# Gated heads of an HGRN2 block: six binary levels of decayed products as three groups of four quarters, and the sums of k and v moved behind a dense panel

## What is computed

```
log_f = log_sigmoid(zf);  k = sigmoid(-zf);  q = silu(zq)
S_t = diag(f_t) S_{t-1} + k_t v_t^T
o_t = S_t^T q_t                # then RMSNorm over the head, times silu(zo)
```

## Time and profile before

| | |
|---|---|
| median of 3 runs | 1657.83 us (1657.72 to 1658.1) |
| the profiled execution | 1658.33 us, of which its span is 1656.6 us |
| busy in the span | PE 1620.1, DVE 837.7, ACT 826.4, POOL 708.4 us |
| stage of the heads | from 103 us to about 345 us |
| one turn of the loop over heads | 32.72 us |

### The profile page before, as it was taken

The page is one execution under the profiler, slowest core; times in us unless marked ns, Lnnn a source line. Parts: engine busy times, 40 slices in busy tenths (PEclk is TensorE's granted clock), DMA queues, the critical chain, the costliest instruction groups (busy, mean ns, idle before and its releaser), DMA issues.

```text
span 1656.6 us, 21578 instructions
## 1 busy us (share of the span) xinstructions
PE 1620.1 (98%) x7677; PEld 1341.8 (81%) x7677; DVE 837.7 (51%) x1279; ACT 826.4 (50%) x1102; POOL 708.4 (43%) x934
## 2 busy tenths in 40 slices
PE   7999999999999999999999999999999999999997
PEld 6888888888888888888887788888888887788875
DVE  3566666631124212121256758358357348679676
ACT  6467777752334313132346645445345355654764
POOL 7453333346666454555565534634635632000000
PEclk9999999999999999999999999999999999999999
DMA  6231221123333333333333222422422313232311
GB/s 206 77 88 52 63 76 57 49 68 106 101 102 102 91 100 101 90 101 94 97 93 85 77 64 76 115 64 77 113 56 81 110 61 88 82 91 81 97 58 61
DMA packets 251096, 142.95 MB, mean 86 GB/s; under 512 B 6161, under 2 KB 249618, under 8 KB 251026
## 3 DMA queue, kind: packets, MB, share of 16 engines
q1 hardware_dynamic: 251026, 142.00, 29.7%
HBM read 139.89 MB, written 2.10 MB: 86 GB/s over the span
## 4 chain that ended last, share of the span: by engine, by line
PE 71%; DVE 6%; ACT 2%; issue 1%; DVEq 0%; ACTq 0%
PE bank L801 19%; PE bank L802 18%; PE bank L809 18%; PE bank L792 2%; PE bank L793 2%; PE bank L794 2%; PE bank L1126 1%; PE bank L1109 1%; PE bank L1108 1%; PE bank L1107 1%; DVE xT L2147 1%; DVE w_lo L2444 1%; PE bank L1252 1%; PE bank L1254 1%; PE bank L1253 1%
## 5 line engine op out<-in xcount | busy, mean ns | idle before, releaser
L772 POOL TENSOR_TENSOR w_lo<-raw,w_hi 128x256 fp32r<-128x256 f32 x896 | 697.3, 811 | 668.8 <-ACT w_hi L1340 668.5
L1340 ACT ACTIVATE w_hi<-raw 128x1024 fp32r<-128x1024 f32 x264 | 277.4, 1055 | 507.8 <-PE bank L809 454.4
L801 PE MATMUL bank<-h_hi,w_hi 128*128 128x512 f32 x1252 | 497.0, 397 | 0.0
L802 PE MATMUL bank<-h_lo,w_hi 128*128 128x512 f32 x1252 | 487.8, 390 | 0.0
L809 PE MATMUL bank<-h_hi,w_lo 128*128 128x512 f32 x1252 | 309.8, 389 | 0.0
L801 PEld LDWEIGHTS bank<-h_hi,w_hi 128*128 128x128 f32 x1252 | 235.1, 188 | 54.2 <-issue 6.0
L802 PEld LDWEIGHTS bank<-h_lo,w_hi 128*128 128x128 f32 x1252 | 235.1, 188 | 52.0 <-issue 4.1
L809 PEld LDWEIGHTS bank<-h_hi,w_lo 128*128 128x128 f32 x1252 | 235.0, 188 | 49.3 <-issue 0.5
L2147 DVE TENSOR_TENSOR xT<-xT,bank 128x512 f32<-128x512 f32 x103 | 68.3, 685 | 205.9 <-PE bank L809 156.9
L2172 DVE SCALAR_TENSOR_TENSOR fr<-bank,rstd 128x512 f32<-128x512 f32 x32 | 22.1, 692 | 133.6 <-PE bank L809 127.9
L801 PE MATMUL bank<-f_hi,w_hi 128*128 128x512 f32 x224 | 87.1, 389 | 0.0
(11 more groups left out here) (430 smaller groups left out, 2711.1 us busy)
## 6 DMA issues: line engine op xcount, KB each, us to landing
raw<-in_w_ff SPq DMA_DIRECT2D x64, 512.0 KB, 4.0
raw<-in_w_in SPq DMA_DIRECT2D x56, 512.0 KB, 3.8
raw<-in_m_w_in SPq DMA_DIRECT2D x48, 512.0 KB, 3.9
raw<-in_r_w_in SPq DMA_DIRECT2D x24, 512.0 KB, 3.8
raw<-in_m_w_out SPq DMA_DIRECT2D x16, 512.0 KB, 3.4
raw<-in_r_w_out SPq DMA_DIRECT2D x16, 384.0 KB, 3.2
raw<-in_w_up_b SPq DMA_DIRECT2D x8, 512.0 KB, 4.1
raw<-in_w_out SPq DMA_DIRECT2D x8, 512.0 KB, 3.9
```

The source lines that it names most:

```text
L772: ins = pool.tensor_tensor(w_lo[:, s, part], raw[:, s, part], w_hi[:, s, part].bitcast(F32), ALU.subtract)
L801: pe.matmul(dst, w_hi[:, s, c], hi[:, k, :], start=(k == 0), stop=False)
L802: pe.matmul(dst, w_hi[:, s, c], lo[:, k, :], start=False, stop=False)
L1340: act.activation(w_hi[:, p % RING, :], raw[:, p % RING, :], ACT.Copy).then_inc(hi_ready[p % RING], 1)
```

## The change

- `GROUPS = [2, 8, 32]` takes the place of the six levels above 1. A group splits an aligned run of 4h tokens into four quarters. The keys of the first three quarters are decayed to the end of their own quarter (`sk`, in place, 384 of 512 columns); of the queries there are three variants side by side (`sq3`): quarters 1 to 3 referred to the end of quarter 0 (3h of 4h columns), quarters 2 and 3 referred to the end of quarter 1 (2h), quarter 3 referred to the end of quarter 2 (h). Together 192 columns in a block.
- PE makes one product of 192 columns for a block in each group, in two parts of two blocks; each part takes a whole bank (`GROUP_BANK`, `GROUP_TURN`). The transposes of `kd` come after the last group.
- DVE writes each part into `sd` with three predicated copies, of 3h, 2h and h columns in each run, under a mask of one byte for a quarter that is broadcast over its columns. 24 copies a head, 10 before.
- The products of `kT` and `vT` are a function of their own, `head_sums`, in bank 6, between the panels 2 and 3 of the next head; `head_states` runs within the next head's `head_prepare`, after its first exponents. The head's output is in bank 4, its sum of squares in bank 5.
- Exponents and exponentials are made in place in `sk`, `sq3` and `kd`; `ee` and `qk` are gone. `sk` is cleared once. The mask tables are smaller.

```diff
-LEVELS = [1, 2, 4, 8, 16, 32, 64]
-NMASK = 8
+GROUPS = [2, 8, 32]
+NG = len(GROUPS)
+N_LEVEL = 2 + 2 * NG
-JOBS = [1, 2, 4, 8, "k", 16, 32, 64, "q"]
+JOBS = [1, 2, 8, "k", 32, "q"]
+GROUP_BANK = {0: (6, 4), 1: (5, 6), 2: (7, 4)}
+GROUP_TURN = {0: (0, 1), 1: (1, 1), 2: (1, 2)}
-H_AUX = {4: 2, 5: 3, 6: 2, 7: 3}
+H_AUX = {4: 4, 5: 4, 6: 3, 7: 2}
...
 # PE
-                for m in range(2, NMASK):
...
-                    pe.wait_ge(qk_made, i * NJ + JOBS.index(h) + 1)
-                    for n in range(NT):
...
-                        mm = pe.matmul(dst.rearrange("p (b t) -> p b t", t=h), qk[:, m - 2, c], right, start=True,
-                                       stop=True, skip_group_check=True)
-                    mm.then_inc(level_done, 1)
-                    if m == 4:
-                        free(5, 1)
...
+                def group(g):
+                    pe.wait_ge(qk_made, i * NJ + JOBS.index(GROUPS[g]) + 1)
+                    for part in range(2):
+                        b = GROUP_BANK[g][part]
+                        free(b, GROUP_TURN[g][part])
+                        for n in range(2 * part, 2 * part + 2):
+                            at = (n - 2 * part) * PAIR
+                            mm = pe.matmul(bank[b][:, at:at + PAIR], sk[:, g, n * P:(n + 1) * P], sq3[:, g, n, :],
+                                           start=True, stop=True, skip_group_check=True)
+                        mm.then_inc(level_done, 1)
+
+                group(0)
+                group(1)
+                group(2)
                 free(5, 2)
+                pe.wait_ge(qk_made, i * NJ + JK + 1)
+                for c in range(NT - 1):
+                    mm = pe.transpose(bank[5][:, c * P:(c + 1) * P], kd[:, c * P:(c + 1) * P], ident[:])
+                mm.then_inc(kd_turned, 1)
+
+            def head_sums(i):
+                aux_released(pe, 6, AUX_H[6] + 2, i, H_AUX[6])
                 pe.wait_ge(kT_made, i + 1)
                 for c in range(NT - 1):
-                    mm = pe.matmul(bank[5][:, c * P:(c + 1) * P], kT[:, c, :], vT[:, c, :], start=True, stop=True,
+                    mm = pe.matmul(bank[6][:, c * P:(c + 1) * P], kT[:, c, :], vT[:, c, :], start=True, stop=True,
                                    skip_group_check=True)
                 mm.then_inc(kv_done, 1)
...
                 head_levels(i)
                 head_in(i + 1, 2)
+                head_sums(i)
                 head_in(i + 1, 3)
                 head_values(i)
...
 # ACT
+                            e = sk[:, g, :].rearrange("p (b c) -> p b c", c=4 * JOBS[j])[:, :, 0:3 * JOBS[j]]
+                            act.activation(e, e, ACT.Exp)
+                            e = sq3[:, g].rearrange("p n c -> p (n c)")
+                            act.activation(e, e, ACT.Exp).then_inc(decay_made, 1)
...
 # DVE, exponent(j)
+                        dve.tensor_tensor(e, c[:, :, :, h - 1:h].to_broadcast([P, S // (4 * h), 3, h]), c, ALU.subtract)
...
+                        for part, dst in variants(sq3[:, GROUPS.index(h)], h):
...
+                            ins = dve.tensor_tensor(dst, later(cn, h, part),
+                                                    end.to_broadcast([P, NT, P // (4 * h), w]), ALU.subtract)
+                        ins.then_inc(expo_made, 1)
...
 # DVE, weigh(j)
+                        dve.tensor_tensor(e, e, blocks(kk[:], h)[:, :, 0:3, :], ALU.mult)
+                        for part, e in variants(sq3[:, g], h):
+                            ins = dve.tensor_tensor(e, e, later(qq, h, part), ALU.mult)
+                        ins.then_inc(qk_made, 1)
                 exponent(1)
                 for j in range(NJ):
+                    if j == 0 and before is not None:
+                        head_states(before)
                     if j + 2 < NJ:
                         exponent(j + 2)
                     weigh(j)
...
 # DVE, head_masks
+                def group(g, part):
...
+                    dve.wait_ge(level_done, i * N_LEVEL + 3 + 2 * g + part)
...
+                    for quarter in range(3):
+                        w = (3 - quarter) * h
+                        dst = sd[:, n:n + 2, :].rearrange("p n (g s) -> p n g s", s=4 * h)[:, :, :, (quarter + 1) * h:]
+                        src = both[:, :, at:at + groups * w].rearrange("p n (g s) -> p n g s", s=w)
...
+                        turn()
+                        ins = dve.copy_predicated(dst, mask, src)
+                        if quarter < 2:
+                            ins.then_inc(mask_turn, 1)
+                            turns += 1
+                            dve.wait_ge(mask_turn, i * M_TURNS + turns)
+                    ins.then_inc(aux_free[b], 1)
+                    if (g, part) != (NG - 1, 1):
+                        dve.wait_ge(aux_free[b], AUX_H[b] + GROUP_TURN[g][part] + 1 + i * H_AUX[b])
```

More of the change, by code:

```diff
@@ L963, in head_sum @@
             def head_sum(i):
[L964 removed]
+                aux_released(pe, 5, AUX_H[5] + 3, i, H_AUX[5])
                 pe.wait_ge(hsq_made, i + 1)
[L966 removed]
+                pe.matmul(bank[5][:], ones[:], hsq, start=True, stop=True).then_inc(hss_done, 1)
             def up(i, n):
@@ L1927, in _ @@
             dve.tensor_copy(mask_d[:], maskf[:, 0:1, :])
-            for n in range(NT):
-                dve.tensor_copy(mask4[:, 1:, n * 64:(n + 1) * 64], maskf[:, 1:, 0:64])
+            dve.tensor_copy(mask4[:, 0:NMASK, :], maskf[:])
             for n in range(NT):
@@ L1983, in head_prepare, with variants, later @@
                 link(dve.tensor_tensor_scan(cum[:], keep[:], lf[:], 0.0, ALU.mult, ALU.add))
+                def variants(t, h):
+                    g = P // (4 * h)
+                    at = 0
+                    for part in range(3):
+                        w = (3 - part) * h
+                        yield part, t[:, :, at:at + g * w].rearrange("p n (g s) -> p n g s", s=w)
+                        at += g * w
+                def later(ap, h, part):
+                    return ap.rearrange("p n (g s) -> p n g s", s=4 * h)[:, :, :, (part + 1) * h:4 * h]
                 def exponent(j):
@@ L2079, in head_masks @@
-                assert turns == M_TURNS
+                for g in range(NG):
+                    group(g, 0)
+                    group(g, 1)
+                assert turns == M_TURNS, turns
             def head_states(i):
                 dve.wait_ge(kv_done, i + 1)
-                link(dve.tensor_copy(state[:, 0, :], bank[5][:, 0:P]))
-                link(dve.scalar_tensor_tensor(state[:, 1, :], state[:, 0, :], eq[:, P - 1:P], bank[5][:, P:2 * P],
+                link(dve.tensor_copy(state[:, 0, :], bank[6][:, 0:P]))
```

165 lines of the change are left out of this document (68 added, 97 removed).

## The result

The changed kernel takes 1678.32 us as a median (1677.35 to 1678.67 in 4 runs), 1.0122 of the kernel before (95% interval 1.0109 to 1.0135). The forecast was 1679.6, in a range from 1667 to 1690. The profiled execution has a span of 1676.3 us against 1656.6.

The account below looks back on a forecast made before the run. PE, busy 32.47 of a head's 32.72 us, was taken as the bound. Seven steps at +2.3 us (16.1) plus +5.7 in the last head gave +21.8 us: 1679.6 us as a median, range 1667 to 1690.

Parts of the forecast that it names:

- PE's own work: Level products on PE: 48 passes (5.21 us) become 24 (3.8 us), 1.4 us less in a head.
- The masks: DVE's copies into sd: 18 short for six, a part 1.46 us (1.63 at h = 2) with gaps, ending at 13.0.
- Dear copies: Rival on DVE's masks: each of the 18 copies takes 0.445 us, a part 1.87; 1690 us, chance 0.12.
- cheap masks: Rival on DVE's masks: no gap between copies, parts 0.93 to 1.1 us; 1661 us, chance 0.05.
- PE's stalls in the levels: PE waits in the groups for banks that DVE's copies must free: 2.9 us a head, longest 0.95.
- The rival that never waits: In the levels: copies keep up with PE, whose whole saving of 1.4 us a head comes out; 1647 us, chance 0.04.
- the rival of a slow clock in each head: Stalls in the levels drop PE to half clock in each head, +11 us more; 1691 us, chance 0.06.
- The chain behind the transposes: Late kT and POOL beside DVE's exponents delay ACT's square; sum of squares at 28.85 instead of 26.49, +2.3 us a head.
- no contention: Rival on the chain: POOL misses or little slows the exponents, PE's order sets the pace; 1674 us, chance 0.11.
- The sum: Whole kernel: 16.1 us for seven heads plus 5.7 for the last, +21.8 us, 1679.6 as a median.
- The last head: Head 7: nothing stands between masks and values, so PE waits for the copies until 14.5; one time +5.7 us.
- late work on PE alone: PE's work before the sum of squares ends 1.78 us later, less the 0.25 it waited anyway: +1.5 us a head.

Follow-up runs that it names:

- one copy a part: Changed kernel making only the first of the three predicated copies in each part of a group, leaving the output incomplete; 1660.43 us, ratio 1.0018.
- the upper halves late: Changed kernel with ACT's two w_hi copies of this stretch moved behind the square and behind the root; 1671.69 us, ratio 1.0081.
- the square early: Changed kernel with only ACT's square of the head's values moved ahead of an exponential of the next head; 1675.39 us, ratio 1.0108.
- the sums back: Changed kernel with the products of kT and vT put back behind the groups, before panel 2 of the next head; 1679.48 us, ratio 1.0129.
- the two versions with all edits and the square early: Changed kernel, k's transposes and w_hi moved, square early, last head's sum straight behind its values: 1660.62 us; likewise with farthest group on ACT: 1659.68 us.
- farthest group on ACT: All three edits plus the h=32 group put first and copied into sd by ACT without masks; 1664.98 us, ratio 1.0046.
- panels in the last head: Changed kernel with one more panel product before the last head's sums and values and one before its sum of squares; 1681.24 us, ratio 1.014.
- all three edits: Changed kernel with k's transposes behind the first group, ACT's w_hi behind the square, and panels in the last head; 1663.95 us, ratio 1.0037.

## Why the prediction was right, step by step

**PE's own work.** Forecast 1.4 us less in a head; 1.3 measured in the run with one copy a part. No run cashed it.

**The masks.** Forecast parts of 1.46 and 1.63 us, measured 1.42 and 1.56; the end of the masks at 13.0, measured 12.9; kd's transposes at 8.75, measured 8.72. Dear copies and cheap masks, the two rivals about this price, are both out. The gaps of 0.15 and 0.23 stand between the short copies as they stood between the long ones: at h = 2 three copies with the two gaps between them take 1.32 and the part 1.56. The rule of the Trainium skill ("VectorE: DVE Perf Modes", The DRAIN you can't avoid), by which a semaphore after each instruction costs nothing over one after the last, speaks of giving a signal. Here each copy also waits for the signal of the one before, so the prediction stretched the rule when it let the gaps fall away by it. No run has these copies without semaphores, so the rule itself wasn't tried.

**PE's stalls in the levels.** Forecast 2.9 us, the longest 0.95; measured 3.1 and 0.88. The rival that never waits is out with this. The granted clock was 1.00 in the turn shown, so the rival of a slow clock in each head is out. What it allowed for once, behind the last head's wait, did happen: 1.7 us of full speed are gone there, where the 3 us at half clock that the prediction assumed would have been 1.5. The forecast had left it out of the sum.

**The chain behind the transposes.** kT forecast at 9.45, measured 9.37. The end of the first exponents forecast at 19.8, measured 157.03 - 136.85 = 20.2: POOL's piece began at 16.4 and hit all four subtractions and not three. The sum of squares forecast at 28.85, measured 28.68. The run with the upper halves late gave the turn 1.06 us back, which is against the rival "no contention".

**The sum.** Forecast 2.3 us a head, measured 2.13; 16.1 for seven, measured 14.9. The last head forecast at +5.7, measured +5.36 to the end of the state products. That it comes so close is in part luck: the copies ended at 13.9 and not 14.5, and the products of the values and the states took 2.92 and not 2.55, at the lower clock.

**What was wrong in it, though the number came out.** The prediction named the square, late at the sum of squares, as the one place where late masks reach PE. The run with the square early shows a second path of nearly the same length: masks, exponents, ACT's queue, root, `o_lo`, the next head's masks. It is a ring through DVE and ACT with PE hanging on it, and in the changed kernel's trace it closes without slack, 34.86 us from a head's first copy (138.61) to the next one's (173.47): copies to the one that frees the bank of k's transposes (145.45); transposes and kT (from 146.22); ACT to the end of the logarithm (150.69); DVE without a pause to the third group's subtractions (163.24); ACT without a pause to the end of the root (170.31); then `hf`, `o_hi`, `o_lo`, each as soon as the one before is done. PE's products have a part in it only with k's transposes. The sum of squares has none: it is made at 165.53, and ACT comes to the root only behind `w_hi` and a table load, at 167.68. Of the 2.1 us a turn only 0.5 goes away when the square does; the run with the sums back shows the same from the other side, as its PE wait of 1.04 us cost nothing. The assumption that the root and the next masks "follow as now" gave the right size because both paths are late by about the same (the sum by 2.19 us in the turn, the root by 2.20). The two expectations that treated a PE wait as a term of the sum (the sums back, the square early in the changed kernel) missed by 4.5 and 4 to 6 us.

One reading was wrong without harm to the sum. PE's wait at the sum of squares was taken as 0.25 us; the row says 0.64. With that, late work on PE alone is worth 1.78 - 0.64 = 1.1 us a head and not 1.5, and the rival "no contention" comes to 1671.5 us and not 1674. The run that takes POOL away measured 1671.69, its turn 1.10 us over the kernel before.

The last head's cause was named rightly (the copies: without them the rest is +0.4), but the remedy tried first was not, since it delayed the sum of squares on which the root hangs.

**What stays open.** No run keeps POOL's subtraction off the first exponents and leaves ACT's queue as it is; that the gain of the upper halves late is POOL's is read from a trace and not shown by a run. Nor is it known why the clock falls behind some waits and not behind others. A third question is why the two versions with all edits and the square early keep 2.4 us (farthest group on ACT) and 3.0 us of loss behind the start of the last head: `o_hi` is a weight 2.7 and 1.8 us later after that start than in the kernel before, with a wait of 1.39 and 1.38 us for `o_lo`, but the chain there wasn't taken apart, and the other 1.2 us of the second lie behind it.

## What to carry to other kernels

Fewer and larger products for TensorE are no gain when another engine must then empty the banks in more pieces: here 1.3 us less on PE was bought with 14 more copies a head, of about 0.5 us each with their gaps. Price a part on the slower side, with its gaps, before counting passes.

When a loop is a ring through several engines, a wait on the busiest one isn't a term to be taken off: follow the ring until it closes and price its whole length, then ask which edit shortens it. And look in each in-order queue for an early-ready item that stands behind late ones. One such item, the square, was worth 0.2% to the kernel as it stood; no version with the groups was faster than the kernel before.

## What the runs showed of the hardware

- A predicated copy from PSUM under a byte mask costs about 0.18 us and 1.04 ns an element, down to short ones: 192 elements alone take 0.37 to 0.39 (one copy a part, h = 8 and 32), and 192, 128 and 64 with their two inner gaps 1.18 to 1.21. With runs of two columns the element costs more (parts at h = 2: 1.32).
- A DVE subtraction of 384 elements with both inputs in SBUF takes 0.55 us alone and 0.99 beside POOL's subtraction; POOL's four pieces take 3.64 us then, 2.84 without such company. Both engines lose.
- ACT copies 32 rows of 192, 128 and 64 elements out of PSUM in 0.83 us for the three, DVE's masked copies of the same part take 1.20. PE stood for them all the same.
- Behind a wait in the last head the granted clock fell to half in eight of the fourteen kernels, in one profiled execution each, and gave away 1.7 or 3.4 us. The wait does not settle it: behind the same wait of 3.90 us for `o_lo` it fell in "panels in the last head" and "all three edits" and stayed at 1.00 in "farthest group on ACT".
- Busy PE time was 32.47 us with 183 matmuls and 32.43 with 159 in a turn. It doesn't tell work from waiting at this grain; the gaps in the weight loads do.
